# Outputs of a state scan from 32-column maps on four column groups of the array, with the rotated sums made in PSUM

## What is computed

```
b_re = cf_re * bu_re - cf_im * bu_im          # u times B, per group of 16 channels
b_im = cf_re * bu_im + cf_im * bu_re
s    = scan over t of  s[t] = (ab_re + i ab_im) * s[t-1] + b[t]
y    = einsum('blgp,ghp->blgh', s_re, C_re) - einsum('blgp,ghp->blgh', s_im, C_im) + D_skip * u
```

## Time and profile before

| | us |
|---|---|
| median of 3 runs | 3112.78 (3111.28 to 3113.39) |
| span of the profiled execution | 3111.9 |
| PE busy in it | 3051.9 (98%) |
| DVE busy | 2004.1 (64%) |
| ACT busy | 1524.5 (49%) |
| the scan's stretch | about 2595 to 2920 of the span |

### The profile page before, as it was taken

The page is one execution under the profiler, slowest core; times in us unless marked ns, Lnnn a source line. Parts: engine busy times, 40 slices in busy tenths (PEclk is TensorE's granted clock), DMA queues, the critical chain, the costliest instruction groups (busy, mean ns, idle before and its releaser), DMA issues.

```text
span 3111.9 us, 44644 instructions
## 1 busy us (share of the span) xinstructions
PE 3051.9 (98%) x16190; PEld 2622.1 (84%) x16190; DVE 2004.1 (64%) x2333; ACT 1524.5 (49%) x1991; POOL 76.4 (2%) x124
## 2 busy tenths in 40 slices
PE   9999998999999999999998999999999999999999
PEld 8899887888888888898887888888888798788887
DVE  6467856555555555667756666556665667888664
ACT  6545546444444444645546455555554554444543
POOL 0000100000000000000100000000000200000000
PEclk9999999999999999999999999999999999999999
DMA  7655554665656555554554666666665545666555
GB/s 268 215 170 168 181 177 143 218 192 191 190 185 194 192 192 183 174 174 161 186 173 156 209 217 205 199 208 216 204 213 191 171 164 196 193 208 211 172 187 172
DMA packets 174363, 592.68 MB, mean 190 GB/s; under 512 B 26941, under 2 KB 32249, under 8 KB 171897
## 3 DMA queue, kind: packets, MB, share of 16 engines
q1 hardware_dynamic: 150784, 545.33, 53.8%
q10 hardware_dynamic: 20968, 32.67, 3.2%
q0 software_dynamic: 2464, 12.67, 1.3%
HBM read 573.79 MB, written 17.07 MB: 190 GB/s over the span
## 4 chain that ended last, share of the span: by engine, by line
PE 87%; DVE 6%; ACT 2%; DVEq 2%; issue 1%; DMA 1%; ACTq 0%; POOL 0%; POOLq 0%; SPq 0%
PE acc L697 22%; PE acc L698 22%; PE acc L699 22%; PE acc L705 5%; PE acc L708 4%; PE acc L707 4%; DVE lo L1771 2%; PE tp L743 1%; PE tp L1111 1%; DVE sr L2520 1%; PE tp L773 1%; ACT hi L1168 1%; DMA raw<-in_stream 1%; DVEq L2541 1%; PE tp L888 0%
## 5 line engine op out<-in xcount | busy, mean ns | idle before, releaser
L1771 DVE TENSOR_TENSOR lo<-raw,hi 128x1024 fp32r<-128x1024 f32 x1032 | 1245.7, 1214 | 832.1 <-ACT hi L1168 822.0
L1168 ACT ACTIVATE hi<-raw 128x1024 fp32r<-128x1024 f32 x1032 | 1078.2, 1050 | 1223.7 <-PE acc L699 996.8
L697 PE MATMUL acc<-hi,xh 128*128 128x512 f32 (+2 forms) x2512 | 976.9, 389 | 8.5 <-issue 6.6
L699 PE MATMUL acc<-hi,xl 128*128 128x512 f32 (+2 forms) x2512 | 968.4, 386 | 0.0
L698 PE MATMUL acc<-lo,xh 128*128 128x512 f32 (+2 forms) x2512 | 968.1, 385 | 0.0
L697 PEld LDWEIGHTS acc<-hi,xh 128*128 128x128 f32 x2512 | 473.5, 188 | 103.5 <-issue 8.0
L699 PEld LDWEIGHTS acc<-hi,xl 128*128 128x128 f32 x2512 | 472.9, 188 | 94.3
L698 PEld LDWEIGHTS acc<-lo,xh 128*128 128x128 f32 x2512 | 473.5, 189 | 90.6
L705 PE MATMUL acc<-xh,hi 128*128 128x256 f32 x1152 | 332.6, 289 | 3.6 <-issue 2.4
L708 PE MATMUL acc<-xh,lo 128*128 128x256 f32 x1152 | 326.5, 283 | 0.0
L707 PE MATMUL acc<-xl,hi 128*128 128x256 f32 x1152 | 326.5, 283 | 0.0
(11 more groups left out here) (411 smaller groups left out, 2603.2 us busy)
## 6 DMA issues: line engine op xcount, KB each, us to landing
raw<-in_stream SPq DMA_DIRECT2D x1032, 512.0 KB, 4.2
turn_scratch<-made ACTq DMA_DIRECT2D x8, 1024.0 KB, 6.8
gpost<-in_post_g POOLq DMA_DIRECT2D x6, 1024.0 KB, 5.3
rotc<-turn_scratch ACTq DMA_DIRECT2D x8, 512.0 KB, 4.8
rots<-turn_scratch ACTq DMA_DIRECT2D x8, 512.0 KB, 7.3
u_stack<-u_scratch ACTq DMA_DIRECT2D x24, 128.0 KB, 4.4
y<-in_mem SPq DMA_DIRECT2D x4, 512.0 KB, 7.8
h<-in_x ACTq DMA_DIRECT2D x4, 512.0 KB, 7.1
```

The costliest lines, as they stand in the source:

```text
L697: nc.tensor.matmul(o, ah, high, start=first, stop=False)
L699: last = nc.tensor.matmul(o, al, high, start=False, stop=final)
L1168: nc.scalar.activation(hi[s][:, :, 0:w], raw[s][:, :, 0:w], ACT.Copy).then_inc(hi_done, 1)
L1771: nc.vector.tensor_tensor(lo[s][:, :, 0:w], raw[s][:, :, 0:w], hi[s][:, :, 0:w].bitcast(F32), ALU.subtract).then_inc(split_done, 1)
```

## The change

The maps are stored as they are, 32 columns for each tile j (`cmap`, 128 x 4 x 32). The two sums of `forward` are not made on DVE. Each of the four products is multiplied by its map instead, and PSUM adds the four: real map by `sd[0]` and by `st`, imaginary map by `sd[1]` and by `sr[1]`. So that both real products are added, `st` is made with a factor of -1 by a scalar_tensor_tensor in place of a tensor_tensor. Each matmul has 128 rows and 32 columns, at a tile position of 32 j columns, and writes 32 partitions of PSUM; there are 16 for a chunk instead of 8, with j running fastest. `states` is incremented after the fourth product. The clearing of `cpad` and its semaphore go.

```diff
-        scan += [(6.8 + 0.6 * n, "forward", c, n) for n in range(6)]
+        scan += [(6.8 + 0.6 * n, "forward", c, n) for n in range(4)]
...
-        cpad = [at_offset(f"cpad{n}", r_at + 36864 + 2560 * n, [P, 5 * P]) for n in range(2)]
+        cmap = [at_offset(f"cmap{n}", r_at + 36864 + 512 * n, [P, 4, 32]) for n in range(2)]
...
                     o = take_turn(pe, pos, STP[f"s{c}_y"])
-                    for j in range(4):
-                        for m in range(2):
-                            last = nc.tensor.matmul(o[:, 0, :], cpad[m][:, j * P:(j + 1) * P], sd[m][:, j, :],
-                                                    start=j == 0 and m == 0, stop=j == 3 and m == 1)
+                    terms = ((0, sd[0]), (0, st), (1, sd[1]), (1, sr[1]))
+                    for n, (m, turned_) in enumerate(terms):
+                        for j in range(4):
+                            last = nc.tensor.matmul(o[32 * j:32 * j + 32, 0, :], cmap[m][:, j, :], turned_[:, j, :],
+                                                    start=n == 0, stop=n == 3, tile_position=(0, 32 * j))
                     last.then_inc(tp_full, 1)
...
-                    act.dma_start(cpad[m][:, :].rearrange("p (j w) -> p j w", w=160)[:, :, 0:32],
-                                  map_scratch[:, m, 4 * c:4 * c + 4, :]).then_inc(maps_loaded, 16)
+                    act.dma_start(cmap[m][:, :, :], map_scratch[:, m, 4 * c:4 * c + 4, :]).then_inc(maps_loaded, 16)
...
-                        act.wait_ge(maps_cleared, 1)
...
-            for m in range(2):
-                last = nc.vector.memset(cpad[m][:, :], 0.0)
-            last.then_inc(maps_cleared, 1)
...
                     elif n == 1:
-                        nc.vector.tensor_tensor(st[:, :, :], sr[1][:, :, :], sin_, ALU.mult)
+                        nc.vector.scalar_tensor_tensor(st[:, :, :], sr[1][:, :, :], -1.0, sin_, ALU.mult, ALU.mult)
                     elif n == 2:
                         nc.vector.tensor_tensor(sd[1][:, :, :], sr[0][:, :, :], sin_, ALU.mult)
-                    elif n == 3:
+                    else:
                         nc.vector.tensor_tensor(sr[1][:, :, :], sr[1][:, :, :], cos_, ALU.mult)
-                        dve.drain()
-                    elif n == 4:
-                        nc.vector.tensor_tensor(sd[0][:, :, :], sd[0][:, :, :], st[:, :, :], ALU.subtract)
-                    else:
-                        nc.vector.tensor_tensor(sd[1][:, :, :], sd[1][:, :, :], sr[1][:, :, :], ALU.add)
                         dve.drain().then_inc(states, 1)
```

## The result

The changed kernel takes 3090.0 us (median; 3088.0 to 3090.7), against 3112.8 before: a ratio of 0.9928, 95% interval 0.9917 to 0.9939. The profiled span is 3088.9 us, 23.0 less than before. In it the part behind the outputs of chunk 7 is as long as before (194.0 us from the tenth matmul behind them), and the stretch from the first `inputs` to that matmul fell from 319.1 to 296.8 us: the gain lies in the scan's stretch.

The account below looks back on a forecast made before the run. TensorE, busy 98% of the span, was taken as the bound, with its gaps. Outputs and switch 8 x (0.22 + 0.54) = +6.1 us, waits -10.5 us, net -4.4 us: 3108.4 us, range 3091 to 3136 (own case 3103 to 3113).

Parts of the forecast that it names:

- part 3: Outputs on TensorE: 32 tiled records a chunk, one matmul per 0.216 us, 3.67 us instead of 3.46, +0.22 a chunk.
- Rival 2: Outputs: all four column groups work at once, 1.73 us a chunk, 3093 us in all; chance 0.22.
- two cases (order, no order): Outputs on TensorE: program order, 3.67 us a chunk, or all four groups at once despite the order, 1.73 us.
- Part 4, the switch: Entering and leaving the tiled form around outputs: between 0 and 0.54 us a chunk, upper end taken.
- The waits, 10.5 us: Outputs waiting for DVE's drain: 8.1 us waits, 0.8 exposed loads, 1.6 clock fall at chunk 0, all counted as gained.
- What is late next: Split of weight units: its 2.0 us of waits lie mostly ahead of any removed sum and stay.
- Rival 4: Outputs as forecast, but units split late as PE runs ahead of DVE: perhaps 3 us gained, 3116 us; chance 0.06.
- Rival 1: Outputs: no overlap of 32-column matmuls, 32 records take 6.91 us a chunk, 3134 us in all; chance 0.23.
- Rival 3: Outputs: group loads not hidden behind running matmuls, 32 records take 10.4 us a chunk, 3162 us; chance 0.06.
- Part 2, the small edits: Product with factor -1 (1219 ns against 1218), memsets, map loads and turns: nothing gained or lost.

Follow-up runs that it names:

- two groups at a time: Changed kernel with column groups 0 and 1 taking turns through all four terms, then groups 2 and 3: 3096.2 us, ratio 0.9951.
- The run without the sums: Kernel before with forward's two sums left out of the computation, padded full-width matmuls of sd[0] and sd[1] unchanged: 3099.9 us, ratio 0.9966.
- the groups alone: Kernel before with 32-column maps on four column groups, the two sums staying on DVE, 8 matmuls a chunk: 3091.6 us, ratio 0.9939.
- changed again: The changed kernel itself, timed again beside three versions built on it: 3087.9 us, ratio 0.9920.
- mixed: Changed kernel with the sums in PSUM for chunks 0 to 3 only, on DVE for chunks 4 to 7: 3088.3 us, ratio 0.9928.
- values: Changed kernel with the window attention's values product as 64-column maps on two column groups taking turns: 3087.7 us, ratio 0.9922.
- mixed with values: Changed kernel with sums in PSUM for chunks 0 to 3 only and the values product on two column groups: 3083.0 us, ratio 0.9902.
- the sums at full width: Kernel before with the sums made in PSUM by 16 padded full-width matmuls a chunk, no column groups: 3127.8 us, ratio 1.0057.
- one group at a time: Changed kernel with the loop order swapped, all four terms of one column group in a row, then the next group: 3110.3 us, ratio 0.9999.
- full-width matmuls between or at the end: Changed kernel plus four unread full-width matmuls a chunk, one after each term (3111.7 us) or all behind the tiled ones (3103.1 us).
- the run with `skip` moved: The mixed with values kernel with skip ahead of the next chunk's first back operation on DVE: 3083.6 us, ratio 0.9906.

## Why the prediction was wrong

**The step that failed is in part 3: "the two records of one matmul need the same column group. So they can't overlap each other", hence one matmul per 0.216 us.** The first half is right (in each group the second record starts 0.24 us after the first), the conclusion isn't. I assumed that an instruction which has to wait for its group holds up the next one. The runs with one and with two groups at a time show that about four records of a group can be out at once. So record 2 of matmul j waits in its group while record 1 of j + 1 begins in another, and with j fastest all four groups fill. 32 records take 8 distances instead of 17: 1.73 us and not 3.67, 1.94 us a chunk, 15.5 us in all. This is most of the miss of 18.4 us. Rival 2 had the right term for the outputs, with the doubt that two records of one group stand between; that was no obstacle. Having no row on the point, I put two cases (order, no order) and no case between, a queue for each group.

**Part 4, the switch: mechanism right, size off.** 0.54 us a chunk was taken, the upper end; measured 0.33. That is 1.7 us less in eight chunks. In the rows of chunk 5 it is the 0.32 us from the last full-width start to the first tiled one, where 0.23 is the usual distance, and the rest behind the tiled ones.

**The waits, 10.5 us: right.** The run without the sums gave 11.6 us, with an interval of some 4 us either way. In the trace of the kernel before, the distances from start to start around the seven waits are 9.0 us longer than usual, and the fall of the clock costs 1.6 us: 10.6 us. Cover was enough in each chunk, and the clock stays at 1.00 in the three windows above. With the groups alone, the fall of the clock at chunk 0 came back with the wait, as its cause would have it; elsewhere a wait of this size isn't always followed by a fall (last section).

**"What is late next": partly wrong.** I let the splits' 2.0 us stand, as lying mostly ahead of any removed sum. That reading was wrong: only 0.4 us of it lies ahead of chunk 0's sums (at 2628.5), 1.4 us lies at 2669 and 0.2 us at 2714. By the distances from start to start, exposed loads included, the splits cost 3.4 us before and 1.5 after. DVE's relief by itself isn't the cause: the run without the sums still has 1.9 us of them on PE's side. In exchange 1.0 us of `inputs` waiting for `skip` is new, in a form that I hadn't named: PSUM's tile is freed by DVE behind its first `back` operation, and short outputs bring PE there sooner. The two waits replace each other. In the five profiles in which `inputs` of chunk 1 waits 0.8 to 1.0 us (changed kernel, changed again, mixed, values, mixed with values), the longest wait of a load for a split, some 20 us later, is 0.7 us. In six profiles in which `inputs` waits for nothing it is 1.8 us: the kernel before, the sums at full width, no sums, one group at a time, full-width matmuls between or at the end. In the run with `skip` moved it is 1.8 us too. The last two runs differ in the place of `skip` alone and show the exchange best. So about 1 us of the splits' 1.9 is what PE had already waited at `inputs`; the rest wasn't separated (two groups, 1.2 us, and the groups alone, 0.8, lie between). Rival 4 was of this kind, but its wait replaced one that I had counted as staying, and both together cost less than before.

**The sum mended.** 8 x (-1.73 + 0.33) = -11.2 for the outputs, -10.5 for the waits, -1.9 for the splits, +1.0 for `inputs`: -22.6 us, measured -22.8, and -22.3 in the scan's stretch of the profiled executions. The terms come from the same profiles, and the interval of the time reaches from 19 to 26 us, so an agreement this close is partly chance.

**The rivals.** Rival 1 (one after the other) is what full-width records do (3127.8 us with the sums in PSUM); tiled ones don't. The argument for it, that the distance is always the moving columns over the clock, doesn't hold in its own rows: it is 0.216 us for 256 columns of plain fp32 and 0.23 us for 512 of fp32r. Rival 3 (loads in the open) fell: loads of four groups go out 0.16 us in total and run beside the matmuls:

```profile
2819.40 0.16 PEld L1111 LDWEIGHTS tp<-sd,cmap 128*32 128x32 f32 x8 [0.35 <-issue]
2819.65 0.35 PEld L1111 LDWEIGHTS tp<-st,cmap 128*32 128x32 f32 x8
```

All 32 loads use all rows, and from the second one on they run while a matmul does, as the full-width loads did in the earlier trace rows. The Trainium skill (TensorE: Matmul & The Clock Gate, Part 3, The mechanism) says that loads overlap running matmuls only when the row group differs, though it also names a background weight buffer as a way around that. The trace disagrees with the bare rule; whether there is such a buffer, no run here shows.

The eight starts of a later row lie within 0.23 us (0.61 - 0.38), two levels 0.216 us apart, which leaves some 0.02 us for three steps; the trace has the first four starts at 0, 7, 14 and 20 ns. The few ns between column tiles that the Trainium skill (TensorE: Matmul & The Clock Gate, Measured speedup vs the span model) gives, about 4, are of this order.

The Trainium skill (TensorEngine Tiling (Array Packing), Key Properties) has TensorE drained when the tiling mode changes. The 0.33 us of a round trip are compatible with it; that it is a drain isn't shown.

**Part 2, the small edits:** the product with -1 takes 1220 ns against 1218, and nothing else of them shows.

## What to carry to other kernels

Where a stationary operand is padded with zeros to 128 columns, cut it to its own columns and give each piece its column group, with the groups in the innermost loop: four groups cost the time of one, and one excursion into that form costs a third of a microsecond. The runs show it in the time for 256 moving columns in plain fp32; with 128 moving columns on two groups the records got shorter, and the time doesn't show it clearly. Once matmuls are this cheap, a sum on a late vector engine can be bought for a matmul in PSUM, but only where that engine is waited for; elsewhere the matmuls cost 0.86 us a chunk by their distances and gain nothing (the times of the mixed version are too close to show this). When no row shows how a new form is queued, take the full overlap as seriously as none, and put a case between them.

## What the runs showed of the hardware

- Plain fp32 matmuls (two records each) on four column groups run four side by side at 0.216 us for 256 moving columns, the same distance as one at full width: 3.46 us for 16 records became 1.73 for 32.
- Order inside the tiled form matters by steps, through what each group can hold: groups taking turns 1.55 us from first to last start of a chunk, pairs 2.44, one group after the other 4.2. The kernel times were 3090, 3096 and 3110 us. In both slower orders the next group began with the fifth of eight records of the one before.
- Out of and into the full-width form: 0.33 us for a round trip. The first tiled record starts 0.09 us later than a full-width one would, the rest is lost behind the last.
- At chunk 0 a wait of 2.41 us on TensorE (kernel before) and one of 2.14 us (groups alone) were each followed by 3.4 us at half the clock, granted share 0.50. Without the wait the clock stayed up there, also through the tiled matmuls. A wait of this size doesn't always do it: the 2.1 us at 107 us of the span, which every kernel has, are followed by such a fall in the second profile of the changed kernel and not in the first, nor in that of the kernel before.
